# First block: the differential attention passes between the plain passes of the two tiles, and the result turned chunk pair by chunk pair inside the passes

## What is computed

```python
p = h @ w_in; pc = hc @ w_in[:, some columns]     # 256 tokens, 256 context tokens
ya = window_sink_attn(qa, ka, va, ka_c, va_c, sink)   # 8 heads of 64, a sink in the softmax: "plain"
yb = chunk_gmlp(u, v, ws, bs, gtok)                   # gelu(u) * (ws @ norm(gelu(v)) + bs)
w  = softmax(q1 k1) - lam * softmax(q2 k2)            # 4 heads of 32: "differential"
yc = rmsnorm(w @ v, gsub) * (1 - lam_init)
y  = concat(ya, yb, yc) @ w_out                       # 512 + 256 + 256 channels
x  = x + gt1 * y                                      # gt1 from silu(c) @ w_ada
```

## Time and profile before

| | |
|---|---|
| runs, median (lowest to highest) | 2089.19 us (2086.98 to 2090.71), 3 runs |
| profiled execution, its own time | 2087.08 us |
| its span | 2085.3 us |
| PE busy | 1952.7 us (94%) |
| DVE busy | 1376.6 us (66%) |
| ACT busy | 994.6 us (48%) |
| GpSimd (POOL) busy | 83.0 us (4%) |

### The profile page before, as it was taken

How to read it: one execution, slowest core, us unless ns; L and a number is a source line. 1 busy time by engine, 2 the same in 40 slices (tenths; PEclk the granted TensorE clock), 3 DMA queues, 4 the chain that set the end, 5 groups by cost and what they waited for, 6 DMA issues and landing times.

```text
span 2085.3 us, 29878 instructions
## 1 busy us (share of the span) xinstructions
PE 1952.7 (94%) x12658; PEld 1737.9 (83%) x12658; DVE 1376.6 (66%) x1467; ACT 994.6 (48%) x1159; POOL 83.0 (4%) x105
## 2 busy tenths in 40 slices
PE   7998869999997899999999899999999999989998
PEld 3977768888886899999877799989998998768997
DVE  4888558999996687666434587768765553365444
ACT  3344337777775333354445443344334553535432
POOL 1330000000000000000000000000001000000000
PEclk9988979999999899999999999999999999999999
DMA  8555328999995587545312477757864442124554
GB/s 354 230 217 193 148 98 331 372 347 353 359 365 220 218 305 290 217 182 206 147 72 81 162 290 295 277 208 285 300 222 142 182 182 82 61 101 170 195 182 152
DMA packets 63877, 458.42 MB, mean 220 GB/s; under 512 B 7040, under 2 KB 7296, under 8 KB 8832
## 3 DMA queue, kind: packets, MB, share of 16 engines
q1 hardware_dynamic: 63744, 456.51, 58.1%
HBM read 455.43 MB, written 1.05 MB: 219 GB/s over the span
## 4 chain that ended last, share of the span: by engine, by line
issue 79%; DVE 7%; PE 6%; DMA 3%; ACT 2%; POOL 1%; DVEq 1%; POOLq 0%; ACTq 0%; SPq 0%
DMA ada<-in_ada 2%; DVE acc L328 2%; DVE wlo L282 2%; PE PS L355 1%; PE PS L356 1%; PE PS L357 1%; ACT whi L276 1%; DMA raw<-in_stream 1%; PE PS L1196 1%; POOL Z L487 1%; DVE hlo L464 1%; ACT Z L443 0%; DVE acc L322 0%; DVE sm L1704 0%; DVE Z L459 0%
## 5 line engine op out<-in xcount | busy, mean ns | idle before, releaser
L282 DVE TENSOR_TENSOR wlo<-raw,whi 128x2048 fp32r<-128x2048 f32 x282 | 647.0, 2296 | 354.8 <-ACT whi L276 349.6
L276 ACT ACTIVATE whi<-raw 128x2048 fp32r<-128x2048 f32 x282 | 538.5, 1913 | 383.4 <-PE PS L357 344.8
L355 PE MATMUL PS<-whi,hhi 128*128 128x256 f32 (+1 forms) x1616 | 528.4, 327 | 36.5 <-DVE wlo L282 12.3
L356 PE MATMUL PS<-wlo,hhi 128*128 128x256 f32 (+1 forms) x1616 | 516.3, 320 | 0.0
L357 PE MATMUL PS<-whi,hlo 128*128 128x256 f32 (+1 forms) x1616 | 516.3, 319 | 0.0
L355 PEld LDWEIGHTS PS<-whi,hhi 128*128 128x128 f32 x1616 | 317.9, 197 | 62.8 <-issue 15.0
L357 PEld LDWEIGHTS PS<-whi,hlo 128*128 128x128 f32 x1616 | 317.3, 196 | 19.1
L356 PEld LDWEIGHTS PS<-wlo,hhi 128*128 128x128 f32 x1616 | 318.2, 197 | 17.6
L355 PE MATMUL PS<-hhi,whi 128*128 128x256 f32 x1152 | 326.6, 284 | 2.2 <-DVE mod L350 2.2
L357 PE MATMUL PS<-hhi,wlo 128*128 128x256 f32 x1152 | 326.0, 283 | 0.0
L356 PE MATMUL PS<-hlo,whi 128*128 128x256 f32 x1152 | 326.0, 283 | 0.0
(11 more groups left out here) (376 smaller groups left out, 1815.5 us busy)
## 6 DMA issues: line engine op xcount, KB each, us to landing
raw<-in_stream SPq DMA_DIRECT2D x285, 1024.0 KB, 4.9
ada<-in_ada SPq DMA_DIRECT2D x92, 1024.0 KB, 4.9
ada<-in_stream SPq DMA_DIRECT2D x48, 1024.0 KB, 5.1
raw<-in_ada SPq DMA_DIRECT2D x3, 1024.0 KB, 15.3
xs<-in_x SPq DMA_DIRECT2D x1, 1024.0 KB, 11.5
Z<-in_ada SPq DMA_DIRECT2D x1, 1024.0 KB, 19.2
Z<-in_ctx SPq DMA_DIRECT2D x1, 1024.0 KB, 11.4
masks<-in_masks SPq DMA_DIRECT2D x2, 512.0 KB, 9.6
```

The source lines that it names most:

```text
L276: nc.scalar.activation(whi[:, s], src, ACT.Copy).then_inc(hi_ready, 1)
L282: nc.vector.tensor_tensor(wlo[:, s], src, whi[:, s].bitcast(F32), ALU.subtract).then_inc(lo_ready, 1)
L355: nc.tensor.matmul(out_, ah, bh, start=start, stop=False, skip_group_check=check)
L356: nc.tensor.matmul(out_, ah, bl, start=False, stop=False, skip_group_check=check)
```

## The change

The order of the passes becomes 0 to 7, 16 to 31, 8 to 15 (`ORDER1`), so that all differential passes lie between the plain passes of the two tiles. The turns of the differential queries and keys go to iterations 3, 4, 5, 7, 8, 9, the two projected units with their splits to 10 to 14, the GELU to 20 and the gated product to 26; the steps per iteration are laid out anew, with the same sum of 80. Both differential finishes are inside the loop. The result is turned in four pairs of chunks with an own bank each (`Y1_PAIRS`): pair 0 (gated MLP) in iteration 30, pair 1 (differential) in 32, the gate's spreading in 33, pairs 2 and 3 (plain) behind the output projection's first unit of tile 1. The stream brings the units of the output weights in that order. The diagonal of the gate and one plain key buffer move to a part of `zr` that is free then (`ZW`), and the diagonal is made on GpSimd before the loop is far.

```diff
+        ZW = nc.alloc_sbuf_tensor_at("ZW", [P, 1536], F32, offset=zr_at)
...
+        ORDER1 = [*range(0, 8), *range(16, 32), *range(8, 16)]
+        Y1_PAIRS = ((4, 7), (6, 7), (0, 2), (2, 3))
...
-        ATT_STEPS = [4, 5, 3, 5, 2, 3, 3, 0, 3, 3, 3, 2, 0, 3, 1, 3, 3, 3, 3, 2, 3, 2, 3, 3, 3, 3, 3, 1, 2, 2, 1, 0]
+        ATT_STEPS = [4, 5, 3, 5, 4, 3, 3, 3, 3, 3, 3, 2, 3, 3, 0, 3, 3, 0, 3, 2, 2, 3, 0, 3, 1, 3, 3, 1, 1, 3, 2, 0]
...
-        B_TURNS = {0: (6, 0), 1: (6, 1), 3: (7, 0), 4: (7, 1)}
-        C_TURNS = {6: 6, 8: 7, 10: 8, 13: 9, 15: 10, 17: 11}
-        B_CONVS = {2: 9, 5: 10}
-        GELU_TURN, GM_TURN = 10, 19
+        C_TURNS = {3: 6, 4: 7, 5: 8, 7: 9, 8: 10, 9: 11}
+        B_TURNS = {10: (6, 0), 11: (6, 1), 13: (7, 0), 14: (7, 1)}
+        B_CONVS = {12: 9, 15: 10}
+        GELU_TURN, GM_TURN, Y1_TURNS = 20, 26, {30: 0, 32: 1}
...
                 if i in B_TURNS:
                     u, tile = B_TURNS[i]
-                    if i == 3:
-                        pe.wait_ge(*proj_out.at(FILL[6, "x"]))
+                    if tile == 0:
+                        pe.wait_ge(*(t1_out.at(len(TURNS) - 1) if u == 6 else proj_out.at(FILL[6, "x"])))
...
+                if i in Y1_TURNS:
+                    if i == 30:
+                        pe.wait_ge(*yb_done.at(0))
+                    else:
+                        pe.wait_ge(*y1_lo.at(0))
+                        pe.wait_ge(*o_out.at(2))
+                    y1_turn(Y1_TURNS[i])
+                if i == PASSES + 1:
+                    gate_pe(pe, N1, 0, 0, 0, diag1)
...
-            pe.wait_ge(*o_out.at(3))
-            turn(pe, y1_turned, xn, 0, DC)
-            gate_pe(pe, N1, 0, 0, 4)
-            pe.wait_ge(*N1.row.at(0))
             pe.wait_ge(*ada_out.at(EARLY_HALVES - 1 - PE_HALVES))
-            pe.wait_ge(*y1_lo.at(3))
-            out_product(pe, 8, 0, y1_half, lambda: norm_pe(pe, N1, 2, 0, 0, xn, TB))
+            pe.wait_ge(*y1_lo.at(1))
+            u = unit(pe, 8)
+            for t in (1, 0):
+                for kk in range(2):
+                    ins = rows_product(u, kk, hhi[:, 4 + kk], hlo[:, 4 + kk], 4, kk == 0, False, False, (t,))
+                if t:
+                    pe.wait_ge(*o_out.at(3))
+                    y1_turn(2)
+                    y1_turn(3)
...
+            def y1_split(j):
+                c, bank = Y1_PAIRS[j]
+                act.wait_ge(*y1_turned.at(j))
+                nc.scalar.activation(hhi[:, c:c + 2].rearrange("p c n -> p (c n)"), PS[:, bank], ACT.Copy).then_inc(*y1_hi.up)
...
-            split_act(act, y1_turned, y1_hi, 0, 4, 0)
-            gate_act(act, N1, 0, 0, 4)
+                if i >= 31:
+                    y1_split(i - 31)
+            act.wait_ge(*o_out.at(2))
+            gate_act(act, N1, 0, 0, 0)
+            y1_split(2)
+            y1_split(3)
...
-                if i % 8 == 3 and i >= 8:
-                    finish(i // 8 - 1)
-                if i == 28:
+                if i % 8 == 3 and 8 <= i < PASSES:
+                    finish((0, 2, 3)[i // 8 - 1])
+                if i in (20, 28):
                     finish_var()
-                if i == 29:
-                    finish_scale(2)
+                if i in (22, 30):
+                    finish_scale(2 + i // 30)
+                if i in (32, 34):
+                    y1_low(i // 2 - 16)
...
-            finish(3)
-            finish_var()
-            finish_scale(3)
-            gate_dve(dve, N1, mod1[:, 16:24], 1.0)
-            split_dve(dve, y1_hi, y1_lo, 0, 4, 0)
+            finish(1)
+            y1_low(2)
+            y1_low(3)
...
-    seq += list(tall(w_out))
+    t_out = tall(w_out)
+    seq += [t_out[i] for i in (2, 3, 0, 1)]
```

More of the change, by code:

```diff
@@ L492, in gate_pe @@
                 o = (c % 4) * P
-                ins = nc.tensor.matmul(PS[:, bank + c // 4, o:o + P], ones, diag[:, c], start=True, stop=True)
+                ins = nc.tensor.matmul(PS[:, bank + c // 4, o:o + P], ones, to[:, c], start=True, stop=True)
             ins.then_inc(*N.row_mm.up)
@@ L1233, in pe_block1, with y1_turn @@
                     half_sum(pe, u + 1, 6 + (u + 1) % 2)
+            def y1_turn(j):
+                c0, bank = Y1_PAIRS[j]
+                for c in range(2):
+                    for t in range(NT):
+                        o = c * 256 + t * P
+                        ins = nc.tensor.transpose(PS[:, bank, o:o + P], xn[:, t, (c0 + c) * P:(c0 + c + 1) * P], ident)
+                ins.then_inc(*y1_turned.up)
             def turn_pair(i, bank):
@@ L1309, in pe_block1 @@
                     ins.then_inc(*gm_mm.up)
-            pe.wait_ge(*o_out.at(3))
-            turn(pe, y1_turned, xn, 0, DC)
-            gate_pe(pe, N1, 0, 0, 4)
-            pe.wait_ge(*N1.row.at(0))
-            pe.wait_ge(*ada_out.at(EARLY_HALVES - 1 - PE_HALVES))
-            pe.wait_ge(*y1_lo.at(3))
-            out_product(pe, 8, 0, y1_half, lambda: norm_pe(pe, N1, 2, 0, 0, xn, TB))
+                if i in Y1_TURNS:
[7 more added lines that the diff above has]
+                    gate_pe(pe, N1, 0, 0, 0, diag1)
+            pe.wait_ge(*ada_out.at(EARLY_HALVES - 1 - PE_HALVES))
+            pe.wait_ge(*y1_lo.at(1))
[7 more added lines that the diff above has]
+                    y1_turn(3)
+            ins.then_inc(unit_used, 1)
+            for t in range(NT):
+                for w in range(1, 4):
+                    if t == 0:
+                        pe.wait_ge(*y1_lo.at(w))
+                    c = Y1_PAIRS[w][0]
+                    u = unit(pe, 8 + w)
+                    for kk in range(2):
+                        ins = rows_product(u, kk, hhi[:, c + kk], hlo[:, c + kk], 4, False, w + kk == 4, False, (t,))
+                    if t:
+                        ins.then_inc(unit_used, 1)
+                    if t and w == 2:
+                        norm_pe(pe, N1, 2, 0, 0, xn, TB)
+                if t == 0:
+                    ins.then_inc(*y1_half.up)
             norm_pe(pe, N1, 2, 0, 1, xn, TB)
@@ L1543, in pool_block1 @@
             ins.then_inc(*zeros_made.up)
[L1544 to L1546 removed]
+            gate_pool(pool, N1, 0, 0, diag1)
             for t in range(NT):
@@ L1550, in pool_block1 @@
                                         ALU.pow).then_inc(*yc_scale.up)
-            gate_pool(pool, N1, 0, 0)
+                if t == 0:
+                    pool.wait_ge(*var_done.at(0))
+                    nc.gpsimd.tensor_tensor(vstat[:, 8:16], vstat[:, 0:8], k1[:, K1["half"]][:, 0:1].to_broadcast([P, 8]),
+                                            ALU.pow).then_inc(*vn_scale.up)
             norm_pool(pool, N1, 2, 0)
@@ L1699, in finish_scale, with y1_low @@
                                         ALU.mult).then_inc(*o_out.up)
+            def y1_low(j):
+                c, bank = Y1_PAIRS[j]
+                dve.wait_ge(*y1_hi.at(j))
+                nc.vector.tensor_tensor(hlo[:, c:c + 2].rearrange("p c n -> p (c n)"), PS[:, bank],
+                                        hhi[:, c:c + 2].bitcast(F32).rearrange("p c n -> p (c n)"),
+                                        ALU.subtract).then_inc(*y1_lo.up)
             for i in range(PASSES + 3):
```

63 lines of the change are left out of this document (34 added, 29 removed).

## The result

The changed kernel takes 2097.94 us (median of 6 runs, 2095.7 to 2101.4), the kernel before 2087.64 (6 runs, 2086.98 to 2090.71): ratio 1.0047, 95% interval 1.0035 to 1.006, so some 10 us slower. The profiled execution took 2100.65 us, 2.7 above its median; its span is 2098.9 us against 2085.3.

What follows compares the result with a forecast made beforehand. VectorE bounds the first block's attention passes; a chain without a bounding engine sets the tail. +2.4 + 12.8 - 1.7 - 7.9 = +5.6 us gave 2092.7, plus 2.1 for the median 2094.8; range 2085.5 to 2101.

Steps and rivals of the forecast that it cites:

- The tail, -7.9: After the last maximum, which starts at t: output projection starts at t + 7.6 instead of t + 16.4, net -7.9 us.
- that the new tail runs at half clock: Rival, after the last maximum: sum, turns, value products and gate take twice as long, tail gives only 2.6 us; 2100, chance 0.10.
- More work in the passes, +2.4: VectorE in the passes: second differential finish comes inside, 3.9 us; plain finish, sink sum and minimum leave; net +2.4 us.
- because the load is later: GpSimd's gate product at about 122 us: slows VectorE's steps by at most 0.9 us, put at 0.
- New waits for scores, +12.8: Passes 5 to 15: turns and projection tiles in TensorE's queue hold the next scores back, VectorE idles 12.8 us.
- Pass 10 to 11, 4.5: First projection tile waits for ScalarE's four-piece block of pass 10: 7.4 us against 2.9 on VectorE, 4.5 idle.
- the third rival: TensorE's clock falls before or in passes 10 to 15, some 6 us more: 2101, chance 0.11.
- Loads, -1.7: VectorE's waits for conditioning loads in the passes: 6.3 us instead of 8.0, as stalls for TensorE hide the others.
- The new waits don't reach DVE: Rival, passes: no new wait delays VectorE's maxima, only +2.4 and -7.9, loads unchanged; faster, 2083.7, chance 0.13.
- half of them: Rival, passes: half of the new waits reach VectorE, 6.4 us less; 2088.4, chance 0.22.
- The named check for the passes: Last maximum comes 119 to 125 us after the first, 109.5 before; under 115 would mean the sign is wrong.
- that for the longest wait: VectorE's longest idle time ended by TensorE stands before pass 11, about 4.5 us.

Runs made afterwards that it cites:

- the diagonal on ScalarE: Projections back in passes 0 to 5, differential turns in pairs on one bank; against that kernel, ScalarE makes the gate's diagonal instead of GpSimd: 2084.16 us, ratio 0.9982.
- early projections: Changed kernel with projections of units 6 and 7 back in passes 0 to 5, turns on two banks, steps laid out anew: 2083.49 us, ratio 0.9982.
- the kernel with fillers: Changed kernel plus 52 unused 128x128 turns ahead of TensorE's waits in passes 7 to 10: 2094.40 us, ratio 1.0040 to the kernel before.
- the kernel with two banks: Changed kernel with the differential turns alternating between PSUM banks 7 and 5: 2090.37 us, ratio 1.0012 to the kernel before.
- the whole tail: Kernel with early projections and paired turns, all sixteen result turns and the gate's rows put back ahead of the projection: 2092.67 us, ratio 1.0015.
- the kernel with later turns: Kernel with paired turns and the diagonal on ScalarE, its pairs moved from passes 6 and 8 to 7 and 9: 2081.51 us, ratio 0.9975.
- 60 in the whole tail: The whole tail plus 48 unused turns in passes 27 to 32 and 12 ahead of the wait for the result: 2084.38 us, ratio 0.9983.

## Why the prediction was right, and where its sizes were off

The forecast was 2094.8 us, slower, by a loss in the passes and a gain in the tail. The sign and both mechanisms stand: hand-overs and tiles in TensorE's queue hold the maxima back, and the tail is shorter. By the steps, in the profiled execution:

- **The tail, -7.9.** Right. Projection at t + 7.5 (forecast 7.6); from its start to the mark 18.6 us instead of 17.7, the 0.9 for the turns inside. Net -8.1. The rows came in the order and with the lengths that were added up. Two things in it were not seen. The tail before had itself run at half clock: its 16 turns took 3.43 us where 16 take 1.91 at full clock, so 1.5 us of the gain are the clock and not the order. And that the new tail runs at half clock, given 0.10, did not happen in this execution by luck of the instant: the clock was at 0.50 from 232 to 238 us and back in time. Six of the eleven profiles of pieced tails have it in part or in full, so 0.10 was far too low.
- **More work in the passes, +2.4.** Too low in sum, for a reason beside it. VectorE's busy time grew by 3.6 us. With the diagonal on ScalarE (and early projections, the same steps in number) it is 95.7 in one kernel and 96.4 in another, 1.5 to 2.2 above before, so the 2.4 were rather too high for the work that they list; the rest of the 3.6, 1.4 to 2.1, goes with GpSimd's product. I had put this at 0, at most 0.9, "because the load is later": the load wait in pass 1 took back 0.9 of it, but the half freed later came later too, and passes 0 to 4 last 1.3 us longer (21.0 instead of 19.75). The Trainium skill, GPSIMD Engine Reference, section 1 Specifications, says that GpSimd shares its SBUF interfaces with VectorE, with contention when a VectorE instruction has two SBUF inputs. A step reads two; the trace agrees, with 4.63 us for four steps against 3.12.
- **New waits for scores, +12.8 beside the old 2.6.** 15.4 forecast, 18.5 measured. One by one: before maximum 6 1.0 (forecast 1.0), 12 2.1 (2.0), 14 2.3 (2.3), 15 2.1 (2.1); before 10 1.8 (0.85), and one of 1.1 before maximum 5, where the turn of pass 4 waits, which I had not listed. The old 2.6 went away, as their passes moved.
- **Pass 10 to 11, 4.5.** This is the largest term, and mis-sized by 3.6: 8.1 us. The 4.5 were right at full clock, as the kernel with fillers shows with 4.7. The rest, 3.4, is the third rival, the clock in or before passes 10 to 15, given 0.11 and +6 us. It fell at 157 us, ahead of the scores of pass 10, and was back at 171; with the wait before maximum 10 (1.8, and 0.7 in the kernel with fillers) it cost 4.5 in this execution. The forecast itself had the clock at 1.00 there; only its range left room for this.
- **Loads, -1.7.** Wrong in sign, and by 3.7 the term furthest off: +2.0. Of five waits three are as forecast within 0.4, the last was 2.1 instead of 1.0, and the one before maximum 9 3.8 instead of 1.2. A half took up to 7.5 us to land there, against the 4.9 of the earlier trace rows that I used throughout. In the kernels with fillers and with two banks, which have the same steps per pass, it was 2.8 and 1.0, and the last one 0.8 and 0.9, so a part is this execution's.

Sum of the passes: forecast +13.5, measured +21.5; the 8.0 are 1.2 of work, 3.1 of waits for scores, 3.7 of loads. The median is 2.7 us lower than this execution, so against 2087.64 the change is worth +10.3 where I said +5.6. The absolute time was missed by less, 3.1 us, by luck: the forecast had added 2.1 us for the profiled execution of before being below its median, by three runs, and by six runs it is 0.6. Small slips in the prediction's sums (7.5 and not 7.4 before maximum 11, 5.3 and not 5.2 before 14, 6.2 and not 6.3 for the loads) change nothing. The range held, its upper end by 3 us. "The new waits don't reach DVE" and "half of them" are refuted by the waits view. The named check for the passes, 119 to 125 us, was missed by 6; that for the longest wait, about 4.5, by 3.6; the ones for the tail, the hand-over and the later stages held.

What stays open: how often the half clock in pass 10 comes in the changed kernel. One profile has it, and that execution has the lowest mean clock of the six, 0.956; three of the six, from 2098.2 to 2101.4 us, are at 0.956 to 0.959, the three from 2095.7 to 2097.7 at 0.962 or 0.963. So the profile is no typical run in this. It is open where the runs of 2091 us or more of the whole tail lose their time. And no experiment changed the loads alone, so how much of the half clock and of the waits for scores goes back to the late load before maximum 9 isn't shown: in the kernel with two banks that load wait was 1.0, and the clock held as well.

## What to carry to other kernels

Ask of each wait that is put into an in-order queue what stands behind it: here six turns of under 0.7 us each, in one bank, with a projection tile behind them, cost 7.6 us by the medians, and a second bank that was free there gave it back. When side work moves on the engine that feeds the bound one, move the bound one's side work with it: eight steps laid elsewhere were worth 5.2 us more in the passes, and 9 by the medians, of which 2.5 are the half clock of the tail in one of the two profiles. Before pricing a stretch in which TensorE will wait, price it at half clock too, and give that case the chance that the waits deserve.

## What the hardware showed that I had not expected

- Adding work can make a kernel faster. 52 unused turns brought 3.5 us by the median, with intervals that overlap, 60 in the whole tail 8.3, with intervals apart. Each time the profile shows the granted clock at 1.00 (2.4 GHz) where it had stood at 0.50 (1.2 GHz) for some microseconds. Before it fell in the changed kernel, TensorE was busy 1.5 and 1.05 of two stretches of 3 us, with a wait of 3.8 us; before it fell in the tail of the kernel with later turns, 1.5 of 3 us, with 1.5 us as the longest wait. The Trainium skill, TensorE: Matmul & The Clock Gate, section HAM oscillation, tells of a loop whose waits for DMAs throttle the array again and again. The trace agrees in the repetition: three times in the passes of the changed kernel, from 157, 212 and 232 us on.
- GpSimd's product of 128 x 1024 elements, 2.1 us long, made four steps of VectorE beside it 1.5 us longer (4.63 instead of 3.12).
- Executions of one program differ by 4 to 15 us. Profiles of these kernels differ also behind the stretch under study: from the mark to the end of the span it is 1823.2 us in one profile, 1829.4 in the changed kernel's, 1832.6 in another, with the same instructions. So a mark inside the trace says more on one stretch than the program's time does.
